# Three plain steps, block sums on the vector engine, and squares summed on the tensor engine in a hybrid decoder layer

## The chip, the cores and the metric

One NeuronCore of a Trainium2 chip runs the kernel in one launch. The metric is the device time of one execution in microseconds. TensorE multiplies, VectorE (DVE) and ScalarE (ACT) work elementwise, GpSimd (POOL) works elementwise too, and SyncE (SP) issues most DMAs. Each engine has its own instruction stream, and the streams meet at semaphores.

## The reference

One layer: a SwiGLU half-step, a mixer, a second SwiGLU half-step and a final RMSNorm, all in float32, for 512 tokens and a model width of 1024.

```python
def rmsnorm(x, w):
    y = x * lax.rsqrt(jnp.mean(x * x, axis=-1, keepdims=True) + EPS)
    return y * w

def swiglu(x, w_gate, w_up, w_down):
    return (jax.nn.silu(x @ w_gate) * (x @ w_up)) @ w_down

x = x + 0.5 * swiglu(rmsnorm(x, ffn1_norm), ...)   # w_gate, w_up: 1024 x 2816
x = x + hybrid_mixer(rmsnorm(x, mix_norm), ...)    # DeltaNet heads and sparse attention heads
x = x + 0.5 * swiglu(rmsnorm(x, ffn2_norm), ...)
y = rmsnorm(x, final_norm)
```

The change touches the start of both feed-forwards and the start of the program. The mixer is only passed through.

## The kernel before

`x` stands transposed in SBUF: 8 tiles k of 128 features by 512 tokens. Every float32 product is made of three passes at full rate: each operand is split into a rounded `hi` and a remainder `lo`, and `three_pass` (lines 572 to 574) adds hi·hi, hi·lo and lo·hi in PSUM. ScalarE makes each `hi` with a copy that rounds, and VectorE each `lo` with a subtraction. For weights these are `act_split_ffn` (L842) and `dve_split_ffn` (L848).

A feed-forward is a fixed list of steps (`ffn_steps`): 22 gate and up steps, each of two output tiles of 128 features, in three parts of 8, 8 and 6, and 4 down steps behind each part. Gate steps have `u` 0, up steps `u` 1. Step s works on half `s % 2` of every ring: the raw weights, `w_hi` and `w_lo`, and four of the eight PSUM banks.

The first `PLAIN` = 2 gate/up steps are **plain**: 2 output tiles by 8 k, 48 products of 128x512. They run on the raw `x` times the norm weights, without the factor 1/rms of each token, which is multiplied into the output later (`dve_plain`, L936). So TensorE can begin before the norm is known. These inputs lie in `act_hi` and `act_lo`, where later the gated result goes.

All other gate/up steps are **block products**: 7 products of half the k by half the tokens in place of 8 (Winograd's form), 84 of 128x256. They need sums of weight blocks, made on GpSimd (`pool_weight_sums`, L862 to L867) and split by ScalarE and VectorE (`act_split_sums` L874, `dve_split_sums` L881), and seven token blocks `hb`: 0, 1, 2 and B12 are quarters of the normed `x` (k low or high, first or second 256 tokens), 3, 4, 5 and 6 sums of them. Each of 0 to 6 is split into `hb_hi` and `hb_lo` of 1024 columns (L667, L671). `hb_hi_home` is the same memory as `hb_hi`, `hb_sum` the same as `hb_lo`, and `w_sum` the same as `w_lo`.

What sets the order at the start of a feed-forward is written out by hand, one list for each engine: `act_ffn_start`, `dve_ffn_start`, `pool_ffn_start`, `pe_ffn_start`. VectorE there makes 16 products of 256 columns for the four quarters (`dve_hr`, L676) and block sum 5 (L716), GpSimd block sums 3, 4 and 6 (L728 to L733) and `hb_lo` 6. VectorE's `hb_lo` 3, 2, 5 and 4 come after the splits of step 2 and the output of step 0. The first block step takes its products in the order 1, 2, 5, 3, 7, 6, 4, which needs the blocks 1, 0, 3, 2, 5, 4, 6. Afterwards `act_ffn`, `dve_ffn` and `pool_ffn` go through the steps, each with the work for the next step's weights ahead of the last step's output.

The norm: ScalarE squares each tile of `x` (L589), GpSimd adds seven of the eight (`pool_sums`, L1017), TensorE sums over the partitions (`pe_norm_sum`, L617), ScalarE takes the root, VectorE the reciprocal, TensorE spreads it over the partitions into bank 7 (`pe_norm_bc`, L630), and ScalarE copies that to `r_sb` (L643). In the first feed-forward, sum and spreading stand behind k = 1 and k = 3 of step 0, in the second behind k = 3 and k = 5.

Before the first product ScalarE and VectorE make, for each k, the square, `act_hi` and `act_lo`; the split of step 0's weights stands ahead of k = 6. ScalarE also issues the DMAs of constants and parameters.

## Time and profile before

| | us |
|---|---|
| median of three timed runs | 1187.64 (1187.3 to 1187.67) |
| the profiled execution's own time | 1181.77 |
| its span | 1180.0 |

| engine | busy us | share |
|---|---|---|
| PE | 1116.3 | 95% |
| PEld | 976.0 | 83% |
| DVE | 783.9 | 66% |
| ACT | 451.1 | 38% |
| POOL | 491.6 | 42% |

The span is the time from the first to the last instruction of the profiled execution. Busy times include no waits. The times of products in the profile overlap, so the distance from the start of one to the start of the next is the better measure of their rate. PEclk is the clock granted to TensorE, as a share of 2.4 GHz.

### The profile page before, as it was taken

What the parts mean: (1) busy time and instruction counts of PE and PEld (TensorE: products, weight loads), DVE (VectorE), ACT (ScalarE), POOL (GpSimd) and SP (SyncE); (2) the same over time, 40 slices, a digit from 0 to 9 for tenths busy, and PEclk for the clock granted to TensorE, in tenths of its full rate; (3) what the DMA queues carried; (4) which work ended last, traced back from release to release, by engine and by line L of the source; (5) the groups of instructions that cost most, each with busy time, mean ns of one, the idle gap of its engine ahead of it and who ended that gap; (6) DMA issues with size and microseconds to landing.
All of it is one profiled execution on the core that took longest, in us unless ns stands there. A gap on an engine that the chain in (4) does not pass through costs nothing.

```text
span 1180.0 us, 20265 instructions
## 1 busy us (share of the span) xinstructions
PE 1116.3 (95%) x8556; PEld 976.0 (83%) x8556; DVE 783.9 (66%) x938; ACT 451.1 (38%) x605; POOL 491.6 (42%) x308
## 2 busy tenths in 40 slices
PE   3889999999999999999999999999599999999996
PEld 2689889988998887877887767887599899989984
DVE  5999458955886566634446387566997379836953
ACT  5444234522434434311124376343543144414431
POOL 3686058704733000313101298423871278306811
PEclk9999999999999999999999899999899999999997
DMA  6223333332332222123111001122133233323221
GB/s 222 67 81 109 106 107 99 103 119 72 108 96 90 95 94 72 38 73 109 37 55 47 8 2 37 37 72 72 65 113 108 75 105 107 119 95 102 74 75 71
DMA packets 33022, 98.45 MB, mean 83 GB/s; under 512 B 3376, under 2 KB 7984, under 8 KB 31280
## 3 DMA queue, kind: packets, MB, share of 16 engines
q1 hardware_dynamic: 31264, 95.95, 24.8%
q10 hardware_dynamic: 1680, 1.39, 0.4%
q8 instruction: 57, 0.93, 0.3%
q14 instruction: 21, 0.17, 0.0%
HBM read 95.24 MB, written 2.10 MB: 82 GB/s over the span
## 4 chain that ended last, share of the span: by engine, by line
PE 85%; DVE 9%; issue 2%; ACT 2%; POOL 1%; DMA 0%; POOLq 0%; DVEq 0%; ACTq 0%
PE bank L572 23%; PE bank L574 23%; PE bank L573 23%; PE bank L1838 3%; DVE hb_lo L671 2%; PE bank L1605 2%; PE bank L1636 2%; PE bank L1621 1%; DVE h_raw L676 1%; PE bank L1896 1%; DVE act_lo L604 1%; DVE w_lo L848 1%; DVE cv L1349 1%; PE bank L617 1%; POOL hb_sum L731 1%
## 5 line engine op out<-in xcount | busy, mean ns | idle before, releaser
L572 PE MATMUL bank<-hb_hi,w_hi 128*128 128x256 f32 x1120 | 316.5, 283 | 22.6 <-DVE hb_lo L671 8.8
L573 PE MATMUL bank<-hb_lo,w_hi 128*128 128x256 f32 x1120 | 315.3, 282 | 0.0
L574 PE MATMUL bank<-hb_hi,w_lo 128*128 128x256 f32 x1120 | 315.3, 282 | 0.0
L572 PEld LDWEIGHTS bank<-hb_hi,w_hi 128*128 128x128 f32 x1120 | 212.3, 190 | 25.8 <-issue 19.9
L573 PEld LDWEIGHTS bank<-hb_lo,w_hi 128*128 128x128 f32 x1120 | 212.4, 190 | 0.2
L574 PEld LDWEIGHTS bank<-hb_hi,w_lo 128*128 128x128 f32 x1120 | 212.5, 190 | 0.0
L572 PE MATMUL bank<-act_hi,w_hi 128*128 128x512 f32 x416 | 166.1, 399 | 20.1 <-DVE w_lo L848 20.1
L842 ACT ACTIVATE w_hi<-raw 128x1536 fp32r<-128x1536 f32 (+1 forms) x68 | 109.8, 1614 | 166.3 <-PE bank L574 162.4
L848 DVE TENSOR_TENSOR w_lo<-raw,w_hi 128x1536 fp32r<-128x1536 f32 (+1 forms) x68 | 163.0, 2397 | 14.2 <-ACT w_hi L842 13.4
L862 POOL TENSOR_TENSOR w_sum<-raw 128x512 f32<-128x512 f32 x40 | 64.4, 1610 | 250.0 <-PE bank L574 250.0
L574 PE MATMUL bank<-act_hi,w_lo 128*128 128x512 f32 x416 | 165.6, 398 | 0.0
L573 PE MATMUL bank<-act_lo,w_hi 128*128 128x512 f32 x416 | 165.6, 398 | 0.0
L881 DVE TENSOR_TENSOR w_lo<-w_sum,w_hi 128x1024 fp32r<-128x1024 f32 x80 | 105.3, 1321 | 30.1 <-POOL w_sum L867 30.1
L874 ACT ACTIVATE w_hi<-w_sum 128x1024 fp32r<-128x1024 f32 x80 | 84.0, 1058 | 85.2 <-POOL w_sum L867 73.7
L572 PEld LDWEIGHTS bank<-act_hi,w_hi 128*128 128x128 f32 x416 | 78.9, 190 | 38.9 <-DVE w_lo L848 20.1
L572 PE MATMUL bank<-h_hi,w_hi 128*128 128x512 f32 x264 | 109.4, 414 | 0.0
L999 DVE SCALAR_TENSOR_TENSOR x<-bank,x 128x512 f32<-128x512 f32 x48 | 30.9, 686 | 111.0 <-PE bank L574 111.0
L574 PE MATMUL bank<-h_hi,w_lo 128*128 128x512 f32 x264 | 104.6, 396 | 0.0
L573 PE MATMUL bank<-h_lo,w_hi 128*128 128x512 f32 x264 | 104.5, 396 | 0.0
L574 PEld LDWEIGHTS bank<-act_hi,w_lo 128*128 128x128 f32 x416 | 78.8, 189 | 19.2
L573 PEld LDWEIGHTS bank<-act_lo,w_hi 128*128 128x128 f32 x416 | 78.9, 190 | 18.7
L865 POOL TENSOR_TENSOR w_sum<-raw 128x512 f32<-128x512 f32 x40 | 94.2, 2354 | 0.0
(282 smaller groups left out, 1767.5 us busy)
## 6 DMA issues: line engine op xcount, KB each, us to landing
raw<-in_gate_up SPq DMA_DIRECT2D x44, 1024.0 KB, 5.3
raw<-in_w_in SPq DMA_DIRECT2D x13, 1024.0 KB, 5.0
raw<-in_down SPq DMA_DIRECT2D x8, 1024.0 KB, 5.2
raw<-in_down SPq DMA_DIRECT2D x16, 512.0 KB, 4.2
raw<-in_down SPq DMA_DIRECT2D x8, 768.0 KB, 4.3
raw<-in_w SPq DMA_DIRECT2D x8, 512.0 KB, 3.9
x<-in_x SPq DMA_DIRECT2D x4, 512.0 KB, 5.9
raw<-in_w_out SPq DMA_DIRECT2D x4, 512.0 KB, 4.9
```

Of the source, the lines that this page charges most:

```text
L572: pe.matmul(out_ap, wh, xh, start=first, stop=False)
L573: pe.matmul(out_ap, wh, xl, start=False, stop=False)
L574: return pe.matmul(out_ap, wl, xh, start=False, stop=last)
L671: eng.tensor_tensor(hb_lo[:, b], HB_RAW[b], hb_hi[:, b].bitcast(F32), ALU.subtract).then_inc(ready, 1)
L842: act.activation(w_hi[:, par, 0:cols], raw[:, par, 0:cols], ACT.Copy).then_inc(hi_ready, 1)
L848: dve.tensor_tensor(w_lo[:, par, 0:cols], raw[:, par, 0:cols], w_hi[:, par, 0:cols].bitcast(F32), ALU.subtract).then_inc(lo_ready, 1)
L862: pool.tensor_tensor(S[0], A[3], A[2], ALU.add).then_inc(s_sum, 1)
L865: pool.tensor_tensor(S[2], A[1], A[3], ALU.subtract).then_inc(s_sum, 1)
L874: act.activation(w_hi[:, par, c], w_sum[:, par, c], ACT.Copy).then_inc(s_hi, 1)
L881: dve.tensor_tensor(w_lo[:, par, c], w_sum[:, par, c], w_hi[:, par, c].bitcast(F32), ALU.subtract).then_inc(s_lo, 1)
L999: dve.scalar_tensor_tensor(x[:, k, :], banks[4 * (st.step % 2) + ab][:, :], 0.5, x[:, k, :], ALU.mult, ALU.add).then_inc(x_added, 1)
L1838: mm = pe.matmul(o[ch, q, :], a, b, start=True, stop=True)
```

## The change

It sets `PLAIN` to 3, so step 2 of each feed-forward is plain too, and the first block step is an up step, number 3, with the banks 4 to 7. The token blocks are written in pairs by 8 products of 512 columns, reading the spread norm from PSUM bank 7, not from `r_sb`. All four block sums and all seven `hb_lo` are VectorE's, and `pool_ffn_start` is gone. The hand-written lists get a new order. ScalarE waits for the end of step 2 before it writes the gated result of steps 0 and 1, since step 2 still reads `act_hi`.

The squares of the first norm are no longer added on GpSimd: TensorE sums each over the partitions, 0 to 5 ahead of the first plain product and 6 and 7 inside step 0. The weights of step 0 are split in two halves (k 0 to 3 and k 4 to 7), behind tile 4. Parameters are issued ahead of the constants, and the rest of the constants goes from ScalarE's DMA queue to SyncE's.

```diff
-PLAIN = 2
+PLAIN = 3
...
-HB_ORDER = (1, 0, 3, 2, 5, 4, 6)
+HB_HI_ORDER = (1, 0, 2, 3, 5, 4, 6)
+HB_LO_ORDER = (1, 3, 2, 0, 5, 4, 6)
...
+            if m == 0:
+                if k >= 2:
+                    act.wait_ge(sq_multiplied, k - 1)
+            elif positive(k + SUMMED0[m] - 1):
...
+        def pe_head_sums(pe, ks):
+            for k in ks:
+                if k == 0:
+                    pe.wait_ge(consts_landed, 16)
+                pe.wait_ge(sq_ready, k + 1)
+                mm = sum_up(pe, sq[:, k % 2, :], k == 0, k == KT - 1)
+                mm.then_inc(ss_ready if k == KT - 1 else sq_multiplied, 1)
...
-        def dve_hr(dve, f, out, k0, tok):
+        def dve_hr(dve, f, out, k0):
             dve.wait_ge(r_ready, 2 * f + 1)
             for k in range(KT // 2):
-                dve.scalar_tensor_tensor(out[:, k, :], x[:, k0 + k, tok], norm_w[:, 2 * f, k0 + k:k0 + k + 1],
-                                         r_sb[:, tok], ALU.mult, ALU.mult).then_inc(h_raw_ready, 1)
+                dve.scalar_tensor_tensor(out[:, :, k, :], x[:, k0 + k, :].rearrange("p (h t) -> p h t", h=2),
+                                         norm_w[:, 2 * f, k0 + k:k0 + k + 1],
+                                         banks[7][:, :].rearrange("p (h t) -> p h t", h=2),
+                                         ALU.mult, ALU.mult).then_inc(h_raw_ready, 1)
 
         def dve_hb(dve, f, b):
-            if b in (2, 3, 4, 5):
-                dve.wait_ge(hb_sum_dve, f + 1)
-                if b > 2:
-                    dve.wait_ge(hb_sum_pool, 3 * f + {3: 1, 5: 2, 4: 3}[b])
-            hb_split(dve, f, b, hb_lo_dve)
+            dve.wait_ge(hb_hi_ready, 7 * f + HB_HI_ORDER.index(b) + 1)
+            if b != 1:
+                dve.wait_ge(hb_sum_dve, 4 * f + {3: 1, 2: 2, 5: 3, 4: 4, 6: 4, 0: 4}[b])
+            dve.tensor_tensor(hb_lo[:, b], HB_RAW[b], hb_hi[:, b].bitcast(F32), ALU.subtract).then_inc(hb_lo_dve, 1)
...
+        def dve_hb_sum(dve, f, b):
+            dve.wait_ge(h_raw_ready, f * KT + (KT // 2 if b == 3 else KT))
+            if b in (4, 6):
+                dve.wait_ge(hb_sum_dve, 4 * f + {4: 2, 6: 3}[b])
+            in0, in1, op = {3: (B12, HB_RAW[1], ALU.subtract), 5: (HB_RAW[2], B12, ALU.subtract),
+                            4: (HB_RAW[1], hb_sum[:, 5], ALU.add), 6: (HB_RAW[0], hb_sum[:, 4], ALU.subtract)}[b]
+            dve.tensor_tensor(hb_sum[:, b], in0, in1, op).then_inc(hb_sum_dve, 1)
...
             act_hb(act, f, 1)
+            act_split_ffn(act, st[2])
             act_hb(act, f, 0)
-            act_split_ffn(act, st[2])
+            act_hb(act, f, 2)
             act_hb(act, f, 3)
-            act_hb(act, f, 2)
-            act_split_sums(act, st[2])
+            act_evac(act, st[0])
             act_hb(act, f, 5)
             act_hb(act, f, 4)
-            act_evac(act, st[0])
+            act_split_ffn(act, st[3])
             act_hb(act, f, 6)
+            act_split_sums(act, st[3])
+            act.wait_ge(step_done, splits(st[2].step) + 1)
+            act_evac(act, st[1])
 
         def dve_ffn_start(dve, f):
 
             st = FFN[f]
-            half = KT // 2
             dve_split_ffn(dve, st[1])
             dve_rstd(dve, 2 * f)
-            dve_hr(dve, f, HB_RAW[1], half, T_LO)
-            dve_hr(dve, f, B12, half, T_HI)
+            dve_hr(dve, f, K_HIGH, KT // 2)
+            dve_hr(dve, f, K_LOW, 0)
             dve_hb(dve, f, 1)
-            dve_hr(dve, f, HB_RAW[0], 0, T_LO)
-            dve_hr(dve, f, HB_RAW[2], 0, T_HI)
+            dve_plain(dve, st[0])
+            dve_split_ffn(dve, st[2])
+            dve_hb_sum(dve, f, 3)
+            dve_hb_sum(dve, f, 5)
+            dve_hb_sum(dve, f, 4)
+            dve_hb_sum(dve, f, 6)
+            dve_hb(dve, f, 3)
+            dve_hb(dve, f, 2)
             dve_hb(dve, f, 0)
-            dve.wait_ge(h_raw_ready, 2 * (f + 1) * KT)
-            dve.tensor_tensor(hb_sum[:, 5], HB_RAW[2], B12, ALU.subtract).then_inc(hb_sum_dve, 1)
-            dve_split_ffn(dve, st[2])
-            dve_plain(dve, st[0])
-            dve_split_sums(dve, st[2], 0)
-            dve_hb(dve, f, 3)
-            dve_split_sums(dve, st[2], 1)
-            for b in (2, 5, 4):
-                dve_hb(dve, f, b)
-
-        def pool_ffn_start(pool, f):
-
-            pool.wait_ge(h_raw_ready, 2 * f * KT + KT)
-            pool.tensor_tensor(hb_sum[:, 3], B12, HB_RAW[1], ALU.subtract).then_inc(hb_sum_pool, 1)
-            pool_weight_sums(pool, FFN[f][2])
-            pool.wait_ge(hb_sum_dve, f + 1)
-            pool.tensor_tensor(hb_sum[:, 4], HB_RAW[1], hb_sum[:, 5], ALU.add).then_inc(hb_sum_pool, 1)
-            pool.wait_ge(hb_sum_pool, 3 * f + 2)
-            pool.tensor_tensor(hb_sum[:, 6], HB_RAW[0], hb_sum[:, 4], ALU.subtract).then_inc(hb_sum_pool, 1)
-            hb_split(pool, f, 6, hb_lo_pool)
+            dve_plain_evac(dve, st[1])
+            dve_split_ffn(dve, st[3])
+            dve_hb(dve, f, 5)
+            dve_split_sums(dve, st[3], 0)
+            dve_gated(dve, st[1])
+            dve_hb(dve, f, 4)
+            dve_hb(dve, f, 6)
+            dve_split_sums(dve, st[3], 1)
+            dve_act_lo(dve, st[1])
 
         def pe_hb_wait(pe, f, b):
-            if b == 6:
-                pe.wait_ge(hb_lo_pool, f + 1)
-            else:
-                pe.wait_ge(hb_lo_dve, 6 * f + HB_ORDER.index(b) + 1)
+            pe.wait_ge(hb_lo_dve, 7 * f + HB_LO_ORDER.index(b) + 1)
...
-            sum_after, bc_after = (1, 3) if f == 0 else (3, 5)
+            bc_after = 3 if f == 0 else 4
+            if f == 0:
+                pe_head_sums(pe, range(HEAD_SUMS + 1))
...
+                if f == 0 and st is FFN[0][0]:
+                    pe.wait_ge(first_lo, 1)
+                else:
+                    pe.wait_ge(lo_ready, splits(st.step) + 1)
+                start = st is FFN[f][0]
+                if st is FFN[f][2]:
+                    pe.wait_ge(post_done, 5 * st.n - 5)
...
+                    if f == 0 and start and t == 1 and k < KT - 1 - HEAD_SUMS:
+                        pe_head_sums(pe, (HEAD_SUMS + 1 + k,))
+                    if f and start and t == 1 and k == 2:
                         pe_norm_sum(pe, m)
-                    if st.u == 0 and t == 1 and k == bc_after:
+                    if start and t == 1 and k == bc_after:
                         pe_norm_bc(pe, m)
...
+        def act_split_first(act):
+            act.wait_ge(raw_landed[0], 16)
+            act.activation(first_half(w_hi, 0), first_half(raw, 0), ACT.Copy).then_inc(first_hi, 1)
+            act.activation(first_half(w_hi, 1), first_half(raw, 1), ACT.Copy).then_inc(hi_ready, 1)
+
+        def dve_split_first(dve):
+            dve.wait_ge(first_hi, 1)
+            dve.tensor_tensor(first_half(w_lo, 0), first_half(raw, 0), first_half(w_hi, 0).bitcast(F32),
+                              ALU.subtract).then_inc(first_lo, 1)
+            dve.wait_ge(hi_ready, 1)
+            dve.tensor_tensor(first_half(w_lo, 1), first_half(raw, 1), first_half(w_hi, 1).bitcast(F32),
+                              ALU.subtract).then_inc(lo_ready, 1)
...
+        def sp_consts(sp):
+            for a, b in KEPT_RUNS[1:]:
+                sp.dma_start(consts[:, KEPT_AT[a][0]:KEPT_AT[b][1]],
+                             dram["consts"][:, CONST_AT[a][0]:CONST_AT[b][1]]).then_inc(rest_landed, 16)
+            for c in range(2):
+                ch = slice(c * CHUNK, (c + 1) * CHUNK)
+                neg, lev = [dram["consts"][ch, CONST_AT[n][0]:CONST_AT[n][1]] for n in COMPACT]
+                sp.dma_start(neg_c[ch], neg[:, ch]).then_inc(compact_landed, 16)
+                sp.dma_start(level_c[ch], lev.rearrange("p (l n) -> p l n", n=P)[:, :, ch])\
+                  .then_inc(compact_landed, 16)
...
+                if f == 0 and i == 8:
+                    sp_consts(sp)
...
         def _(act):
             first = CONST_AT["ones"][1]
+            act.dma_start(params[:, :], dram["params"]).then_inc(params_landed, 16)
             act.dma_start(consts[:, 0:first], dram["consts"][:, 0:first]).then_inc(consts_landed, 16)
-            act.dma_start(params[:, :], dram["params"]).then_inc(params_landed, 16)
             for k in range(KT):
-                if k == KT - 2:
-                    act_split_ffn(act, FFN[0][0])
+                if k == HEAD_SUMS:
+                    act_split_first(act)
                 act_square(act, 0, k)
                 act_hp(act, 0, k)
             act_ffn_start(act, 0)
```

## Rows read from the trace of the kernel before

**Rows 1.** The page, part 4: the chain that ended last, shares of the span by engine.

```profile
PE 85%; DVE 9%; issue 2%; ACT 2%; POOL 1%; DMA 0%; POOLq 0%; DVEq 0%; ACTq 0%
```

**Rows 2.** What TensorE waited for in the whole span: total us, times, longest us.

```profile
PE bank L572 <- DVE w_lo L848: 25.2, 3, 20.1
PE bank L572 <- DVE hb_lo L671: 8.8, 7, 2.8
```

**Rows 3.** Windows: stretch, its us, busy us and instructions by engine, PEclk granted clock, DMA.

```profile
47.20:50.30 3.10, 0.21 (x1) 0.01 (x1) 3.10 (x5) 2.46 (x3) 2.86 (x1) 1.00 0.07 9
50.30:54.60 4.30, 4.28 (x24) 4.17 (x24) 4.30 (x2) 3.28 (x3) 4.20 (x2) 0.65 0.69 237
54.60:69.70 15.10, 8.23 (x61) 7.36 (x60) 15.07 (x10) 4.21 (x6) 12.89 (x6) 0.99 0.29 77
825.50:831.10 5.60, 0.00 (x0) 0.00 (x0) 5.60 (x8) 5.02 (x6) 2.81 (x1) 0.89 0.02 4
831.10:836.30 5.20, 5.12 (x24) 5.15 (x24) 5.20 (x2) 4.13 (x4) 4.25 (x2) 0.50 0.54 199
836.30:851.50 15.20, 8.41 (x62) 7.42 (x61) 15.16 (x9) 4.19 (x6) 13.77 (x7) 0.99 0.00 1
852.00:858.00 6.00, 6.00 (x51) 5.86 (x51) 5.86 (x7) 1.52 (x2) 5.28 (x3) 1.00 0.53 175
```

**Rows 4.** Timeline of VectorE, first feed-forward: start us, us, engine, line, operation, count.

```profile
8.81 7.99 DVE L604 SCALAR_TENSOR_TENSOR act_lo<-x,params,act_hi 128x512 fp32r<-128x512 f32 x5 [0.38 <-ACT act_hi L598]
...
21.33 2.28 DVE L848 TENSOR_TENSOR w_lo<-raw,w_hi 128x2048 fp32r<-128x2048 f32 x1
...
31.21 3.25 DVE L676 SCALAR_TENSOR_TENSOR hb_hi_home<-x,params,r_sb 128x256 f32<-128x256 f32 x8 [3.95 <-ACT r_sb L643]
...
35.52 6.93 DVE L676 SCALAR_TENSOR_TENSOR h_raw<-x,params,r_sb 128x256 f32<-128x256 f32 x4
...
46.15 1.21 DVE L716 TENSOR_TENSOR hb_sum<-hb_sum,hb_hi_home 128x1024 f32<-128x1024 f32 x1
47.28 1.74 DVE L848 TENSOR_TENSOR w_lo<-raw,w_hi 128x1536 fp32r<-128x1536 f32 x1
48.95 1.27 DVE L936 TENSOR_TENSOR c_sb<-bank,r_sb 128x512 f32<-128x512 f32 x2
...
56.72 7.82 DVE L671 TENSOR_TENSOR hb_lo<-hb_sum,hb_hi 128x1024 fp32r<-128x1024 f32 x3
```

**Rows 5.** Timeline of VectorE, second feed-forward.

```profile
812.07 3.26 DVE L676 SCALAR_TENSOR_TENSOR hb_hi_home<-x,params,r_sb 128x256 f32<-128x256 f32 x8 [3.96 <-ACT r_sb L643]
...
848.81 2.85 DVE L848 TENSOR_TENSOR w_lo<-raw,w_hi 128x1536 fp32r<-128x1536 f32 x1
```

**Rows 6.** Timeline of TensorE in step 0 of the first feed-forward.

```profile
20.14 0.80 PE L572 MATMUL bank<-act_hi,w_hi 128*128 128x512 f32 x1 [20.14 <-DVE w_lo L848]
...
24.14 0.46 PE L572 MATMUL bank<-act_hi,w_hi 128*128 128x512 f32 x1
...
24.90 0.94 PE L617 MATMUL bank<-consts,sq_sum 128*128 128x1 f32 x8
...
26.60 0.48 PE L572 MATMUL bank<-act_hi,w_hi 128*128 128x512 f32 x1
...
28.78 0.40 PE L572 MATMUL bank<-act_hi,w_hi 128*128 128x512 f32 x1
29.02 0.39 PE L573 MATMUL bank<-act_lo,w_hi 128*128 128x512 f32 x1
```

**Rows 7.** Timeline of ScalarE before the first product; ACTq is its DMA issue.

```profile
0.75 0.40 ACTq L2228 DMA_DIRECT2D consts<-in_consts  x1
...
6.92 0.72 ACT L598 ACTIVATE act_hi<-x,params 128x512 fp32r<-128x512 f32 x1 [1.38 <-DMA params<-in_params]
...
8.07 0.71 ACT L598 ACTIVATE act_hi<-x,params 128x512 fp32r<-128x512 f32 x1
...
14.15 1.90 ACT L842 ACTIVATE w_hi<-raw 128x2048 fp32r<-128x2048 f32 x1
```

**Rows 8.** DMA issues from 0 to 0.9 and 2.6 to 2.9 us: KB, us to landing.

```profile
consts<-in_consts ACTq DMA_DIRECT2D x1, 65.0 KB, 4.3
...
raw<-in_gate_up SPq DMA_DIRECT2D x1, 1024.0 KB, 9.8
```

**Rows 9.** The page, part 5: an operation of VectorE with one PSUM operand.

```profile
L999 DVE SCALAR_TENSOR_TENSOR x<-bank,x 128x512 f32<-128x512 f32 x48 | 30.9, 686 | 111.0 <-PE bank L574 111.0
```

More of the change, by code:

```diff
@@ L574, in three_pass @@
             return pe.matmul(out_ap, wl, xh, start=False, stop=last)
-        SUMMED0 = [m * (KT - 1) for m in range(4)]
+        SUMMED0 = [0] + [m * (KT - 1) for m in range(3)]
+        HEAD_SUMS = 5
         def x_there(m, k):
@@ L793, in gate_up @@
                 def gate_up(i):
-                    if part == 0 and isinstance(i, int) and i == 0:
-                        return
                     for st in ups[:2]:
-                        first = part == 0 and st.u == 0 and isinstance(i, int) and i == PLAIN // 2
+                        first = part == 0 and isinstance(i, int) and 2 * i + st.u == PLAIN
+                        if part == 0 and isinstance(i, int) and 2 * i + st.u < PLAIN:
+                            continue
                         pe.wait_ge(lo_ready, i * 2 + (splits(st.step) + 1))
@@ L1005, in pool_ffn @@
         def pool_ffn(pool, f):
-            pool_ffn_start(pool, f)
-            for st in FFN[f][PLAIN + 1:]:
+            for st in FFN[f][PLAIN:]:
                 if summed(st):
```

87 lines of the change are left out of this document (36 added, 51 removed).

## The prediction

> **What bounds the kernel now.** The chain of waits by engine comes first: TensorE 85%, VectorE 9% [rows 1]. TensorE is the bound, and the chain leaves it where it idles. TensorE's waits say where: 25.2 us for the split weights `w_lo`, 20.1 of them before its first product, and 8.8 us for `hb_lo` [rows 2]. The windows say when [rows 3]. Two stretches are badly filled: 47.2 to 69.7 us, at the start of the first feed-forward, and 825.5 to 851.5 us, at the start of the second. In each one block-product step is done. Such a step has 84 products; 51 started in 6.00 us, 0.118 us each, 9.9 us in all. So of 22.5 us in the first stretch 12.6 are lost, and of 26.3 us (825.3 to 851.6) in the second 16.4. With the late start that is nearly all of TensorE's waiting for VectorE. In both stretches VectorE is busy throughout. The clock adds: after 5.6 us without a product the granted clock was 0.50, which is the 1.2 GHz level, and 24 products took 5.2 us (0.217 each, 2.3 us lost); after 3.1 us idle it was 0.65 on average [rows 3].
>
> **How VectorE's time is made up.** VectorE runs at two prices. With GpSimd idle an operation with both tensors in SBUF takes 1.13 us for 1024 columns (from the start at 46.15 to the next at 47.28) and 1.67 us for 1536. With GpSimd busy, three of 1024 took 7.82 us, 2.6 each; four of 256 columns took 6.93 us, where eight had taken 3.25; the split of 1536 took 2.85 instead of 1.74 [rows 4, 5]. So one GpSimd operation costs VectorE between 1.11 (2.85 - 1.74) and 1.47 us (2.6 - 1.13). I take 1.11, as its row has the 512-column weight sums on GpSimd that will be left. A read from PSUM is not lengthened: two of 512 took 1.27 us amid busy GpSimd [rows 4].
> The Trainium skill, page "SBUF — State Buffer", section "Who interferes with whom", gives the rule: an operation of VectorE with two SBUF inputs and one of GpSimd that reads SBUF shut each other out for a whole instruction, and one with at most one SBUF input is left alone. The trace agrees (2.6 against 1.13 us, and 1.27 us for the two from PSUM). It speaks against this change at one place, since the sums of the first two block steps stay on GpSimd and meet the longest VectorE queue.
>
> **Start of the first feed-forward.** Now the first product starts at 20.14 us [rows 6]. ScalarE's products with the norm weights begin at 6.92, when the parameters landed [rows 7]; VectorE needs 7.99 us for five `act_lo`, with GpSimd adding squares beside it [rows 4]. After: the parameters are issued first. What is first now, at 0.75, took 4.3 us to land, so they land between 5.0 and 6.9 us [rows 7, 8]; I take 6.4. Five rounds of square and product at 1.13 us (6.92 to 8.07 between products [rows 7]) end at about 11.5. The raw weights land at 12.5 (issued at 2.66, 9.8 us [rows 8]), and bound the split: ScalarE does halves of 1024 columns in 0.95 us (half of 1.90 [rows 7]), at 13.5 and 14.4, and VectorE its first half by 14.8. But TensorE must first sum the squares 0 to 5, and square 5 is issued behind both halves: ready at 15.0. Its sum is half of the sixteen records that took 1.70 us (24.90 to 26.60), 0.85 us at the clock of that stretch, twice this at 1.2 GHz [rows 6]. Start 15.9 to 16.7, I take 16.2. Gain 3.9 us. The first nine products now take 4.0 us (20.14 to 24.14), 0.44 each against 0.235 later (28.78 to 29.02), so 1.9 us are lost [rows 6]. Whether sums with one column raise the clock beforehand no row shows: bounds 0 and 1.9 us more gain. I take 0, since waits lie between the sums.
> The sums for squares and the broadcast inside step 0 cost what they did (1.7 and 0.85 us). Step 0 then ends at 16.2 + 11.3 + 1.9 + 2.5 = 31.9 and step 1 at 43.2, against 47.2.
>
> **First feed-forward, steps 2 to 4.** A plain step has 48 products of 0.235 us: 11.3 us, 1.4 more than a block step. In it TensorE waits for nothing, as its weights are split at about 36.4. VectorE's queue: the broadcast norm is in PSUM after k=3 of step 0, 25.9, copied at 26.5 (now 31.2 [rows 4]). Eight products of 512 columns with one PSUM operand cost 0.65 each by the row of 686 ns [rows 9], less the overlap: 5.2 us, against 16 of 256 in now 12.8 us. They end at 31.7; `hb_lo` 1 at 32.9, step 0's output (two from PSUM, 1.2) at 34.1, the weights of step 2 (2.28 [rows 4]) at 36.3, four block sums (4 x 1.14) at 40.9, `hb_lo` 3 and 2 at 43.2. Here GpSimd starts on the sums of step 3, as its buffer is free at the end of step 1. From there: `hb_lo` 0, output of step 1, weights of step 3, `hb_lo` 5, weight-sum split 0, gate product, `hb_lo` 4 and 6, weight-sum split 1: nine entries, 10.8 us of their own (1.13 + 1.25 + 1.67 + 6 x 1.13), and four waits for the sums of step 3 up to 52, then two for those of step 4 (6 x 1.11 = 6.7 us, of which some 0.9 fall beside the PSUM reads). Last split at 59.8. TensorE: step 2 to 54.4, products 1, 2, 5 of step 3 to 58.6, product 3 waits for this split 1.2 us, step 3 ends at 65.4. Its weights for step 4 are then split (65.0). Now step 4 starts at 69.7 + 9.9 = 79.6. Gain 14.2 us, the 3.9 included.
>
> **Second feed-forward.** Norm sum and broadcast come after k=2 and k=4 instead of 3 and 5: one k is 6 products, 1.4 us, so VectorE begins at 810.7, not 812.1 [rows 5]. Step 0 ends as now at 814.0 and step 1 at 825.3, for TensorE comes here without a pause. The same queue: eight products to 815.9, `hb_lo` 1 817.0, output 0 818.3, weights of step 2 820.5, four sums 825.1. It is here 2.2 us further behind step 1's end than in the first feed-forward, so all three `hb_lo` meet GpSimd. The nine entries and `hb_lo` 3 and 2 are 10.8 + 2.3 = 13.1 us, with seven waits of 1.11 20.9: last split at 846.0. TensorE has finished step 2 at 836.6 and products 1, 2, 5 at 840.8: it stalls 5.2 us. That is as long as the 5.6 us after which the clock fell, so 2.3 us more [rows 3]. Its last four products take 5.6, and step 3 ends at 853.9, where now step 4 starts at 851.6 + 9.9 = 861.5: gain 7.6 us.
> **Later steps.** VectorE's work between two weight splits stays what it is (about 9 of 9.9 us), and weights of step 4 are ready before TensorE wants them; I add 0, with 2 us as the other end. The 1.1 MB of constants go from ScalarE's queue to SyncE's, ahead of the raw weights of step 8. SyncE waits there for most of a step, so seven issues of 0.5 us are hidden, the transfer too; without that cover some 3 us. ScalarE loses those issues, worth nothing while it is idle.
>
> **Sum.** 14.2 + 7.6 = 21.8 us from the profiled execution's 1181.77, which gives 1160.0. The median shown is 1187.64, 5.9 above it, and I take the same difference: 1165.9 us.
>
> **Rivals.**
> A. *The second stall is missing*: if GpSimd's sums cost VectorE nothing, seven waits (7.8 us) go, TensorE has no stall and no slow clock in the second feed-forward (5.2 + 2.3 more) and 1.2 less in the first, and with a warm start 1.9: gain 30.5 to 32.4, about 1156 us. Against it: the 2.6 us of [rows 4]. Half of it, if GpSimd's operations come mainly beside PSUM reads: 1161.
> B. *The queue on VectorE gets longer*: at 1.47 us a wait, 13 waits cost 4.7 us more, and steps 4 and 5 start late by 1 us each time: gain 15.1, 1172.5. For it: VectorE has no idle time before either.
> C. *The start is not earlier* because sums at 1.2 GHz hold ScalarE's two square buffers: six at 1.7 us from 6.5 end at 16.7, worth 0.5; with parameters or `ones` landing late, up to 2: 1168.
> D. *Slower*: the sums moved to VectorE become the bound. It takes over three block sums, one `hb_lo` and 512 more weight columns, 5.1 us for each feed-forward. If what slows VectorE in the rows is not GpSimd but its own SBUF traffic, eight products at 1.73 instead of 0.65 and six operations at 2.25 instead of 1.13 add 15.3 us to each queue: 30.6 - 21.8 = 8.8 slower, 1196.4. It decides from about 10.8 us of added queue. Against it: the same operation at 1.13 us with GpSimd idle.
> E. *The change does not do what it says*: in the second feed-forward the squares still go through GpSimd, so there it only moves the norm; that is counted.
>
> **Numbers.** Forecast 0.52, A or its half 0.20, B 0.18, C 0.05, D 0.03, nothing much 0.02. The range 1157.5 to 1174.5 takes in A's nearer part and B. The forecast's own is 1162 to 1170. What a measurement of this kernel can tell from no change is about 0.2%, 2.4 us: faster 0.94, same 0.03, slower 0.03.
>
> **What would show it.** First product near 16.2 us; no idle time of TensorE in step 2 of either feed-forward; VectorE's eight norm products in 5.2 us, block sums at 1.14 each; a wait for `w_lo` from `w_sum` (about 5 us) in the second feed-forward's first block step and about 1 in the first's, with a clock near 0.5 behind the long one. I am wrong if the first product comes after 18 us, if TensorE waits for `hb_lo` there, or if a wait of over 2 us appears in steps 4 to 7.

## The result and the profile after

The changed kernel takes 1173.1 us (median of four, 1170.7 to 1177.3), the kernel before 1187.5 in the same series: ratio 0.989, 95% interval 0.9866 to 0.9913. (Ratios and intervals here are estimated over all executions, so they differ a little from the quotient of the medians.) A second series gave 1173.7 against 1190.1, ratio 0.9875 (0.9846 to 0.9903). It is faster, by 14.4 us where 21.8 were forecast. That is inside the stated range, but 7.2 us above the point and outside the 1162 to 1170 us that the forecast's own terms gave; it is the number of rival B, 1172.5.

The profiled execution took 1177.34 us, the slowest of its series. Its chain of waits by engine, to be read beside [rows 1]:

```profile
PE 89%; DVE 5%; issue 2%; ACT 2%; POOL 1%; DMA 0%; POOLq 0%; DVEq 0%; ACTq 0%
```

What TensorE waited for in the whole span, as total, number of times and longest, beside [rows 2]. The line numbers are the changed kernel's: L917 is the split of weight sums, L621 the sums of squares.

```profile
PE bank L574 <- DVE w_lo L917: 8.4, 2, 5.3
PE bank L621 <- ACT sq L595: 8.0, 2, 7.6
```

VectorE's share of the chain fell from 9 to 5%. All waits for `hb_lo` are gone, and so is the wait of 20.1 us for the first weights. In its place stands one of 7.6 us ahead of the first sum of squares. In the two feed-forwards there are two waits for the second weight-sum split, 3.1 and 5.3 us, one in each.

**The head.** TensorE's timeline ahead of and in step 0 of the first feed-forward, beside [rows 6]; the columns are start and length in us:

```profile
7.57 8.70 PE L621 MATMUL bank<-consts,sq 128*128 128x1 f32 x40 [7.57 <-ACT sq L595]
16.66 1.87 PE L621 MATMUL bank<-consts,sq 128*128 128x1 f32 x8 [0.39 <-ACT sq L595]
18.39 0.77 PE L574 MATMUL bank<-act_hi,w_hi 128*128 128x512 f32 x1
...
30.48 0.58 PE L576 MATMUL bank<-act_hi,w_lo 128*128 128x512 f32 x1
30.90 0.40 PE L574 MATMUL bank<-act_hi,w_hi 128*128 128x512 f32 x1
31.13 0.39 PE L575 MATMUL bank<-act_lo,w_hi 128*128 128x512 f32 x1
```

Forty records of one-column sums took 8.70 us, 1.74 us for each tile of `x`, and so did the sum of square 5. The first product came at 18.39, not 16.2. The products of step 0 stood 0.43 us apart up to 30.48, and 0.23 from 30.90 on: 12 us at 1.2 GHz, where the kernel before had 4. The constants, with the column of ones, were issued second, and landed 6.4 us after their issue at 1.17, which is 7.57, the very start of the first sum, beside [rows 8]. So the sum waited for them, and not for the square that the row names, which ScalarE had made by 6.43.

```profile
params<-in_params ACTq DMA_DIRECT2D x1, 172.5 KB, 5.2
consts<-in_consts ACTq DMA_DIRECT2D x1, 65.0 KB, 6.4
```

**VectorE in both feed-forwards**, beside [rows 4, 5]; its timeline, the last two lines from the second one:

```profile
33.32 2.72 DVE L681 SCALAR_TENSOR_TENSOR hb_hi_home<-x,params,bank 128x512 f32<-128x512 f32 x4 [5.75 <-ACT r_sb L655]
35.95 2.72 DVE L681 SCALAR_TENSOR_TENSOR hb_sum<-x,params,bank 128x512 f32<-128x512 f32 x4
...
59.00 1.23 DVE L917 TENSOR_TENSOR w_lo<-w_sum,w_hi 128x1024 fp32r<-128x1024 f32 x1 [1.26 <-POOL w_sum L903]
...
61.28 4.56 DVE L690 TENSOR_TENSOR hb_lo<-hb_sum,hb_hi 128x1024 fp32r<-128x1024 f32 x2
65.77 2.28 DVE L917 TENSOR_TENSOR w_lo<-w_sum,w_hi 128x1024 fp32r<-128x1024 f32 x1
...
842.20 4.52 DVE L690 TENSOR_TENSOR hb_lo<-hb_sum,hb_hi 128x1024 fp32r<-128x1024 f32 x2
846.64 2.28 DVE L917 TENSOR_TENSOR w_lo<-w_sum,w_hi 128x1024 fp32r<-128x1024 f32 x1
```

Eight norm products take 5.3 us (33.32 to 38.59, 5.2 forecast). `hb_lo` 4 and 6 take 2.28 us each, not 1.13, since GpSimd is at its sums, and the last split another 2.28. In the first feed-forward VectorE even stands idle for 1.26 us ahead of 59.00, for the last of GpSimd's four sums.

TensorE behind the stall of the second feed-forward:

```profile
848.98 0.58 PE L574 MATMUL bank<-hb_hi,w_hi 128*128 128x256 f32 x1 [5.28 <-DVE w_lo L917]
849.35 0.42 PE L575 MATMUL bank<-hb_lo,w_hi 128*128 128x256 f32 x1
```

and windows of the first plain products, of step 2 and of the products behind that stall, with the same columns as [rows 3]:

```profile
18.30:30.20 11.90, 11.90 (x38) 10.06 (x38) 3.97 (x4) 4.64 (x6) 0.00 (x0) 1.00 0.58 178
49.60:60.80 11.20, 11.20 (x50) 9.04 (x49) 9.94 (x8) 4.58 (x5) 9.15 (x4) 1.00 0.08 12
848.90:853.40 4.50, 4.42 (x20) 4.43 (x21) 4.37 (x6) 1.89 (x3) 0.00 (x0) 0.50 0.01 2
```

Step 2 (49.6 to 60.8) has TensorE busy throughout. Behind the stall 20 products take 4.5 us at a clock of 0.50. In the head the same column prints 1.00 although the products stand 0.43 us apart: there the distances must be read, not PEclk.

### The profile page after: what moved, and what is told of

The parts are those of the page before. It is cut to its first block, busy times and chain, and to the rows that moved or that the text cites. A ratio compares the mean times of both kernels' runs of the same rounds, so it can differ in the third digit from the quotient of the medians.

```text
span 1175.5 us, 20165 instructions
## 1 busy us (share of the span) xinstructions
PE 1137.8 (97%) x8532; PEld 993.8 (85%) x8532; DVE 761.5 (65%) x921; ACT 447.8 (38%) x600; POOL 442.6 (38%) x284
## 4 chain that ended last, share of the span: by engine, by line
PE 89%; DVE 5%; issue 2%; ACT 2%; POOL 1%; DMA 0%; POOLq 0%; DVEq 0%; ACTq 0%
PE bank L574 24%; PE bank L575 23%; PE bank L576 23%; PE bank L1890 3%; PE bank L1657 2%; PE bank L1688 2%; PE bank L621 1%; PE bank L1673 1%; DVE hb_lo L690 1%; PE bank L1948 1%; PE bank L1937 1%; PE bank L1944 1%; PE bank L1942 1%; PE bank L1496 1%; PE bank L1316 0%
## 5 line engine op out<-in xcount | busy, mean ns | idle before, releaser
L574 PE MATMUL bank<-hb_hi,w_hi 128*128 128x256 f32 x1064 | 299.8, 282 | 8.4 <-DVE w_lo L917 8.4
L575 PE MATMUL bank<-hb_lo,w_hi 128*128 128x256 f32 x1064 | 299.6, 282 | 0.0
L576 PE MATMUL bank<-hb_hi,w_lo 128*128 128x256 f32 x1064 | 299.6, 282 | 0.0
L574 PEld LDWEIGHTS bank<-hb_hi,w_hi 128*128 128x128 f32 x1064 | 202.0, 190 | 9.1 <-DVE w_lo L917 8.8
L575 PEld LDWEIGHTS bank<-hb_lo,w_hi 128*128 128x128 f32 x1064 | 201.9, 190 | 0.3
L576 PEld LDWEIGHTS bank<-hb_hi,w_lo 128*128 128x128 f32 x1064 | 202.0, 190 | 0.0
L898 POOL TENSOR_TENSOR w_sum<-raw 128x512 f32<-128x512 f32 x38 | 59.0, 1553 | 332.8 <-PE bank L576 332.8
L574 PE MATMUL bank<-act_hi,w_hi 128*128 128x512 f32 x448 | 179.9, 402 | 0.0
L575 PE MATMUL bank<-act_lo,w_hi 128*128 128x512 f32 x448 | 179.2, 400 | 0.0
L576 PE MATMUL bank<-act_hi,w_lo 128*128 128x512 f32 x448 | 179.2, 400 | 0.0
L868 DVE TENSOR_TENSOR w_lo<-raw,w_hi 128x1536 fp32r<-128x1536 f32 (+1 forms) x67 | 159.1, 2374 | 15.2 <-ACT w_hi L862 14.4
L917 DVE TENSOR_TENSOR w_lo<-w_sum,w_hi 128x1024 fp32r<-128x1024 f32 x76 | 101.2, 1336 | 31.0 <-POOL w_sum L903 30.9
L910 ACT ACTIVATE w_hi<-w_sum 128x1024 fp32r<-128x1024 f32 x76 | 80.2, 1058 | 95.6 <-POOL w_sum L903 81.7
L1039 DVE SCALAR_TENSOR_TENSOR x<-bank,x 128x512 f32<-128x512 f32 x48 | 30.9, 686 | 111.0 <-PE bank L576 111.0
L901 POOL TENSOR_TENSOR w_sum<-raw 128x512 f32<-128x512 f32 x38 | 91.8, 2415 | 0.0
```

Source lines behind the costliest of these rows:

```text
L574: pe.matmul(out_ap, wh, xh, start=first, stop=False)
L575: pe.matmul(out_ap, wh, xl, start=False, stop=False)
L576: return pe.matmul(out_ap, wl, xh, start=False, stop=last)
L868: dve.tensor_tensor(w_lo[:, par, 0:cols], raw[:, par, 0:cols], w_hi[:, par, 0:cols].bitcast(F32), ALU.subtract).then_inc(lo_ready, 1)
L898: pool.tensor_tensor(S[0], A[3], A[2], ALU.add).then_inc(s_sum, 1)
L901: pool.tensor_tensor(S[2], A[1], A[3], ALU.subtract).then_inc(s_sum, 1)
```

## Where the time went: three stretches in several profiles

One event each marks the end of step 3 of the first feed-forward (ScalarE's split of step 5's weights, which can't begin before it), the beginning of the second (its split of the weights of step 1), and the end of step 4 of the second (its split for step 6). ScalarE's timeline has them; in the third profile of the kernel before the first two are:

```profile
81.18 1.49 ACT L842 ACTIVATE w_hi<-raw 128x1536 fp32r<-128x1536 f32 x1
...
811.67 1.90 ACT L842 ACTIVATE w_hi<-raw 128x2048 fp32r<-128x2048 f32 x1
```

| profile | execution, us | to the end of step 3 | from there to the second feed-forward | from there to the end of its step 4 |
|---|---|---|---|---|
| before, first | 1181.8 | 80.2 | 723.1 | 68.7 |
| before, second | 1184.3 | 80.0 | 726.8 | 68.7 |
| before, third | 1193.3 | 81.2 | 730.5 | 71.5 |
| changed, first | 1177.3 | 75.6 | 730.5 | 60.9 |
| changed, second | 1170.4 | 70.3 | 730.0 | 60.7 |

The last column fell by 7.8 and 8.0 us from its value in the first two profiles of before (7.6 forecast). The first fell by 4.6 or 9.9 us, where 14.2 were forecast. In the last row ScalarE was late: TensorE began step 4 at 69.27 us there, against 79.95 in the first profile of before, so the gain was 10.7 us; elsewhere in the table the first mark lies 0.3 to 0.4 us behind TensorE. The middle column, in which neither kernel differs but for the DMA queue of the constants, goes from 723 to 730 us in the kernel before alone. A kernel that differs from the changed one in one operand (experiment 9) has 724.1 us there, so the change does not fix that stretch at 730 either. The first profile of before, on which the prediction stood, was the fastest of the three, so the two first profiles' difference (4.4 us) says little. The two gains add up to 12.4 us in the one profile and 18.7 in the other, around the 14.4 of the medians.

## The experiments

All but the kernels before are edits of the changed kernel. The time is a median over the executions of its series, with their least and greatest, and the ratio is to the kernel before in the same series; where only one execution was made, it says so.

**1. The changed kernel again.** No edit.

> The changed kernel once more, for a second profile beside the first. In the first profile the mixer, between about 344 and 677 us, took 6.6 us longer than in the kernel before, though nothing in it was changed. Theory (the difference is the clock's, which falls at other moments from execution to execution): this profile shows another length of that stretch, by some us, while the first feed-forward's start is the same within 2 us. Rival (the change reaches into the mixer, by the constants that SyncE now loads or by its phase): the stretch is again 6 to 7 us longer. Time: 1173 us, 1170 to 1177.

1173.7 us (1170.4 to 1176.7), ratio 0.9875 (0.9846 to 0.9903). TensorE's head in this profile:

```profile
20.96 1.02 PE L621 MATMUL bank<-consts,sq 128*128 128x1 f32 x8
21.84 0.48 PE L574 MATMUL bank<-act_hi,w_hi 128*128 128x512 f32 x1
22.16 0.40 PE L575 MATMUL bank<-act_lo,w_hi 128*128 128x512 f32 x1
```

The clock rose between 20.96 and 21.84 us here, at 30.9 in the first profile, with the same instructions ahead of it. Block step 3 began at 56.0 us instead of 60.6: 4.6 us. Then there is a second difference, behind the same stall of 3.1 us. Windows of 4.5 us from TensorE's next product on, in the first profile and in this one:

```profile
68.10:72.60 4.50, 4.50 (x25) 4.50 (x26) 4.37 (x4) 0.88 (x1) 1.08 (x1) 0.62 0.00 0
```

```profile
63.50:68.00 4.50, 4.47 (x38) 4.47 (x39) 4.37 (x4) 0.84 (x1) 1.12 (x1) 1.00 0.00 0
```

The clock fell behind the stall in the first profile and stayed here, which is 1.5 us more. So TensorE began step 4 at 75.4 us there and at 69.3 here; "the same within 2 us" was wrong. The later profiles show which case is the rule. Of the seven with this head and no added products ahead of the first plain one (the changed kernel twice, experiments 5 to 9), two have the rise at 21 us and five at 30 to 31. The four with the head of before (experiment 3 among them) have it at 24 to 26. The middle stretch was again 6.9 us over the first profile of before, so the rival had to be taken seriously, and the kernel before was profiled twice more.

**2. The kernel before, second and third profile.** No edit.

> The kernel before once more, for a second profile. Its first profile came from an execution of 1181.8 us, while its median is 1187 to 1190; it has no fall of the clock near 580 and 640 us, and five profiles of changed kernels have both. Theory (those falls come and go with the execution, whatever the kernel): this profile, if its time is near the median, shows a granted clock below 1 near 580 and 640 us and a stretch from the last weights of the first feed-forward to the second feed-forward that is 5 to 8 us longer than in the first profile. Rival (the change brings the falls): the stretch is the same as in the first profile within 1 us, and an execution near the median is longer elsewhere.

> The kernel before, a third profile. The second one, 1184.3 us, was longer than the first only in the mixer (3.2 us by 604 us, with a fall of the clock near 590 that the first lacks), and equal to it within 0.5 us in both feed-forwards. Theory: both feed-forwards are again the same within 1 us, and an execution near the median of 1188 us has its difference of 4 to 8 us in the mixer. Rival: the feed-forwards of before differ as well, and then a comparison of single profiles of them says little.

1184.3 and 1193.3 us. The second has 3.7 us more in the mixer, not the 5 to 8 expected, and a fall of the clock near 594 us but none near 640: neither the theory nor its rival as written. It has nothing more elsewhere; the third, unchanged code, has the whole 7.4 us, and 2.8 more in the second feed-forward. So the longer mixer comes and goes without the change. The third profile also refutes "both feed-forwards are the same within 1 us".

**3. The old head.**

```diff
-        SUMMED0 = [0] + [m * (KT - 1) for m in range(3)]
+        SUMMED0 = [m * (KT - 1) for m in range(4)]
...
-            if f == 0:
-                pe_head_sums(pe, range(HEAD_SUMS + 1))
...
-                    if f and start and t == 1 and k == 2:
+                    if start and t == 1 and k == (2 if f else 1):
...
+            pool_sums(pool, 0)
...
-                if k == HEAD_SUMS:
-                    act_split_first(act)
+                if k == KT - 2:
+                    act_split_ffn(act, FFN[0][0])
...
```

> The changed kernel with the head of the program as before: squares added on GpSimd, norm sum behind k=1 of step 0, weights of step 0 split in one piece ahead of tile 6, constants issued ahead of parameters. Theory (one-column sums ran at 1.7 us a tile because TensorE was at 1.2 GHz, and they kept it there until 30.5 us): the first product comes at 20.1 us instead of 18.4, but the clock rises 4 us later, step 1 ends at 47.2 instead of 49.7, and the kernel is 2 to 3 us faster than the changed one, 1170.5. Rival (the late landing of the constants, 7.6 us, is what cost the head its gain, and the clock plays no part): 1.7 us slower than the changed one, 1175.

1170.8 us (1170.0 to 1173.2), ratio 0.985 (0.9824 to 0.9877), 2.9 us under the changed kernel of the same series (1173.7). The first product comes at 20.24, 2 us later, and TensorE begins step 4 at 73.5, 1.9 us before the first profile of the changed kernel and 4.2 behind its second. The time varies over 3.2 us, the changed kernel's over 6.4. The clock rose at 25 us, behind 4.8 us of slow TensorE. The intervals of the two ratios overlap, so that the old head is faster by 2.9 us is not shown; what the series speaks against is the rival, by which it is slower. By the profiles, what the new head wins at the first product it pays at the clock in five of seven executions, and not in the other two.

**4. Dense products ahead of the sums.**

```diff
+        def pe_warm(pe, n):
+            src = z[:, 0, :].bitcast(BF16)
+            for _ in range(n):
+                pe.matmul(banks[7][:, :], src[:, 0:P], src[:, P:P + SEQ], start=True, stop=True)
+
         def pe_head_sums(pe, ks):
             for k in ks:
+                if k == 0:
+                    pe.wait_ge(warm_set, 1)
+                    pe_warm(pe, 20)
...
                 mm.then_inc(ss_ready if k == KT - 1 else sq_multiplied, 1)
+                if k == 4:
+                    pe_warm(pe, 8)
```

> The changed kernel with 20 dense products on a cleared tile ahead of the first sum of squares and 8 behind the fifth; their result is not used. Theory (clock): the sums take 0.85 us a tile, the first product comes at about 16 us and runs at 0.235 us from the start; step 1 ends near 41.5 us instead of 49.7, of which the VectorE queue behind it gives back a part: 5 to 8 us faster than the changed kernel, 1166.5. Rival (constants and raw weights bound the head): the first product stays at 18.4 us and only its 4.3 us of slow products go: 3 to 4 us, 1169. Second rival (a fall of the clock in the head does not depend on what TensorE does there): no change, 1173.

1170.3 us (1164.4 to 1175.4), ratio 0.9833 (0.9798 to 0.9869): 3.4 us under the changed kernel by the medians, with intervals that overlap, and not the 7 expected. TensorE's timeline, and windows of it from 8 us on:

```profile
1.35 6.16 PE L629 MATMUL bank<-z 128*128 128x512 bf16 x20 [1.35 <-POOL z L2280]
7.51 5.97 PE L622 MATMUL bank<-consts,sq 128*128 128x1 f32 x40
13.71 3.19 PE L629 MATMUL bank<-z 128*128 128x512 bf16 x7 [0.24 <-issue]
16.70 1.71 PE L622 MATMUL bank<-consts,sq 128*128 128x1 f32 x8
18.27 0.77 PE L575 MATMUL bank<-act_hi,w_hi 128*128 128x512 f32 x1
```

```profile
8.00:10.00 2.00, 2.00 (x19) 2.00 (x19) 0.81 (x2) 1.43 (x4) 0.00 (x0) 1.00 1.05 389
10.00:12.00 2.00, 1.84 (x14) 1.67 (x14) 1.44 (x2) 2.00 (x4) 0.00 (x0) 0.90 0.99 334
12.00:14.00 2.00, 1.76 (x8) 1.59 (x10) 0.94 (x2) 1.44 (x3) 0.00 (x0) 0.50 0.90 369
```

The dense products did what they should: the five sums behind them take 5.97 us, 1.2 each, ScalarE's pace. But in the midst of the sums the clock fell, 0.90 and then 0.50, though TensorE was busy for 1.84 of 2.00 us. The 8 dense products then ran at half speed and delayed the sixth sum to 16.70, though ScalarE had its square at 15.24, and the first product came at 18.27 all the same. So in this execution one-column sums did not keep the clock up, as the theory has it, and in none of the other profiles had some 10 us of them raised it by the first product. The second rival, a fall that has nothing to do with what TensorE does, is made unlikely by experiment 10 and not excluded. That 28 dense products would repair the head was wrong.

**5. Dense products in the stalls.**

```diff
+                if first and p == 3:
+                    for _ in range(10 if st.f == 0 else 36):
+                        pe.matmul(banks[3][:, 0:TOK], w_hi[:, par, 0:P], hb_hi[:, 1, 0, :], start=True, stop=True)
                 if p in S_PART:
```

> The changed kernel with dense products into an unused bank ahead of the wait for the second weight-sum split: 10 in the first feed-forward (1.2 us of the 3.1 us stall), 36 in the second (4.3 of 5.3 us). Their result is not used. Theory (a stall of that length makes the clock fall, and that costs 1.6 and 2.3 us): the stall in the second feed-forward shrinks to about 1 us, the products behind it run at 0.118 us instead of 0.213, and 2 us are gained in the second, 0 to 1.6 in the first: 1170.5. Rival (the slow products behind the stall come from something else, such as VectorE's writes): same time as the changed kernel, 1173.

1171.3 us (1160.9 to 1173.3), ratio 0.9828 (0.9791 to 0.9866), 2.4 us less than the changed kernel by the medians, which is not clear of the noise; the profile has to decide. TensorE's first two products behind the wait of the second feed-forward, and its wait there:

```profile
846.30 0.39 PE L574 MATMUL bank<-hb_hi,w_hi 128*128 128x256 f32 x1 [1.09 <-DVE w_lo L920]
846.52 0.28 PE L575 MATMUL bank<-hb_lo,w_hi 128*128 128x256 f32 x1
```

```profile
PE bank L574 <- DVE w_lo L920: 1.1, 1, 1.1
```

The wait is 1.1 us, the clock stays, and the last column of the table becomes 59.0, 1.9 us less. In the first feed-forward 10 products filled 1.2 of 3.1 us, and nothing was gained: the clock fell there all the same. The slow products of the second feed-forward belong to the idle time, as forecast: the clock falls behind the stall of 5.3 us in every profile that has it (both of the changed kernel, experiments 3, 4 and 9), and in none of those where it is filled or gone (here, 7 and 10). Behind the 3.1 us of the first it fell in four of five. The time is TensorE's alone; VectorE's queue is as long as it was.

**6. The second split first.**

```diff
             dve_split_sums(dve, st[3], 0)
+            dve_split_sums(dve, st[3], 1)
-            dve_gated(dve, st[1])
             dve_hb(dve, f, 4)
             dve_hb(dve, f, 6)
-            dve_split_sums(dve, st[3], 1)
+            dve_gated(dve, st[1])
             dve_act_lo(dve, st[1])
```

> The changed kernel with VectorE's second weight-sum split of step 3 directly behind the first, ahead of hb_lo 4 and 6 and the gate product. Theory (VectorE's whole queue from the norm to the weights of step 4 is the bound, not the one entry that TensorE waits for): the wait in step 3 goes in both feed-forwards, but the weights of step 4 are split no earlier than before (73.3 and 853.1 us), TensorE waits 5 to 6 us for them, and the clock falls behind that wait: 1 to 3 us faster than the changed kernel, 1171.5. Rival (only the order of the entries is wrong): both stalls (8.4 us) and their slow products (3.9 us) go: 1162.

1174.5 us (1167.3 to 1177.4), ratio 0.9885 (0.9849 to 0.9922): no gain, where 1171.5 was expected. TensorE's only wait at the start of the second feed-forward:

```profile
PE bank L574 <- DVE w_lo L868: 6.6, 1, 6.6
```

L868 is the split of step 4's weights. The wait for the sums is gone, and one of 6.6 us for the next step's weights has taken its place; in the first feed-forward it is 3.2 us, where 3.1 went. The entry that TensorE waited for was not the bound; VectorE's queue as a whole is.

**7. GpSimd's next sums later.**

```diff
             for st in FFN[f][PLAIN:]:
+                if st is FFN[f][PLAIN + 1]:
+                    pool.wait_ge(s_lo, 2 * FFN[f][PLAIN].s + 2)
```

> The changed kernel, but GpSimd begins the weight sums of step 4 only when VectorE has split all sums of step 3. Theory (each GpSimd operation costs VectorE 1.1 us in that queue): hb_lo 4 and 6 and the second split take 1.13 us each instead of 2.25, the stall falls from 5.3 to about 1 us in the second feed-forward and from 3.1 to 0 in the first, the clock stays up behind both, and step 4 starts some 6.8 and 4.5 us earlier; 11 us faster than the changed kernel, 1162. Rival (what is not paid now is paid in step 4, whose sums come later and meet VectorE then): the stalls go, but TensorE waits for sums inside step 4: 2 to 4 us faster, 1170.

1166.8 us (1163.2 to 1170.0), ratio 0.983 (0.9797 to 0.9863): 6 to 7 us under the changed kernel's two medians, where 11 were expected. VectorE in the second feed-forward, and TensorE's waits there:

```profile
835.31 2.35 DVE L690 TENSOR_TENSOR hb_lo<-hb_sum,hb_hi 128x1024 fp32r<-128x1024 f32 x2
837.58 1.22 DVE L917 TENSOR_TENSOR w_lo<-w_sum,w_hi 128x1024 fp32r<-128x1024 f32 x1
...
841.27 2.81 DVE L868 TENSOR_TENSOR w_lo<-raw,w_hi 128x1536 fp32r<-128x1536 f32 x1
...
846.58 2.23 DVE L917 TENSOR_TENSOR w_lo<-w_sum,w_hi 128x1024 fp32r<-128x1024 f32 x1 [1.84 <-POOL w_sum L903]
```

```profile
PE bank L574 <- DVE w_lo L868: 1.4, 1, 1.4
PE bank L574 <- DVE w_lo L917: 1.0, 1, 1.0
```

`hb_lo` 4 and 6 now take 1.13 us each and the split 1.14, with nothing changed on VectorE. That is the price of GpSimd's operations shown by itself: 1.14 us for each entry (2.28 - 1.14). The Trainium skill has the rule for it in "SBUF — State Buffer", section "Who interferes with whom": an operation of VectorE with two SBUF inputs contends with one of GpSimd that reads SBUF. The trace agrees (2.28 against 1.14 us). The rival has its part: the weights of step 4 take 2.81 us, VectorE idles 1.84 us for the late sums, and TensorE waits 1.4 and 1.0 us. The last column of the table is 56.2, 4.6 us less. In the first feed-forward TensorE begins step 5 at 77.6 us, against 79.1 in the second profile of the changed kernel, which has the same head: 1.5 us. Together that is 6.1, near the 6 to 7 measured; TensorE begins step 4 3.1 us earlier and loses half of it there again.

**8. Two block sums on GpSimd again.**

```diff
-            dve_hb_sum(dve, f, 4)
-            dve_hb_sum(dve, f, 6)
...
+            pool.tensor_tensor(hb_sum[:, 4], HB_RAW[1], hb_sum[:, 5], ALU.add).then_inc(hb_sum_pool, 1)
+            pool.wait_ge(hb_sum_pool, 2 * f + 1)
+            pool.tensor_tensor(hb_sum[:, 6], HB_RAW[0], hb_sum[:, 4], ALU.subtract).then_inc(hb_sum_pool, 1)
```

> The changed kernel with block sums 4 and 6 on GpSimd again; all else, the third plain step too, is kept. Theory (a sum that goes to GpSimd saves VectorE 1.13 us but shuts it out for the 2 to 2.5 us that GpSimd needs for 1024 columns): hb_lo 3, 2 and 0 take 2.2 to 3.3 us each, the last weight-sum split comes 2 to 4 us later in each feed-forward, and the kernel is 4 to 7 us slower than the changed one, 1179. Rival (a second engine helps, since VectorE is the bound): 2 x 2.3 us faster, 1168.5.

1178.0 us (1174.0 to 1183.7), ratio 0.9925 (0.9897 to 0.9952), 4.3 to 4.9 us slower than the changed kernel's two medians. VectorE, then GpSimd, in the second feed-forward:

```profile
828.48 4.57 DVE L694 TENSOR_TENSOR hb_lo<-hb_sum,hb_hi 128x1024 fp32r<-128x1024 f32 x2
835.46 2.21 DVE L694 TENSOR_TENSOR hb_lo<-hb_sum,hb_hi 128x1024 fp32r<-128x1024 f32 x1 [2.40 <-POOL hb_sum L1050]
```

```profile
828.63 3.34 POOL L1048 TENSOR_TENSOR hb_sum<-hb_hi_home,hb_sum 128x1024 f32<-128x1024 f32 x1 [19.93 <-DVE hb_sum L700]
832.05 3.27 POOL L1050 TENSOR_TENSOR hb_sum<-hb_sum 128x1024 f32<-128x1024 f32 x1
```

Two sums take GpSimd 6.6 us, 3.3 each, and not 2 to 2.5; VectorE spends 2.28 us on each `hb_lo` beside them and idles 2.40 more for the last. The stall becomes 6.1 us in both feed-forwards, and TensorE begins step 4 2.9 and 2.8 us later than in the first profile of the changed kernel. So the move of these two sums to VectorE is worth some 5 us of the change. What the move of the third sum and of `hb_lo` 6 is worth was not measured.

**9. The norm from SBUF.**

```diff
-                                         banks[7][:, :].rearrange("p (h t) -> p h t", h=2),
+                                         r_sb.rearrange("p (h t) -> p h t", h=2),
```

> The changed kernel with the eight norm products of each feed-forward reading the copy of the spread norm in SBUF and not the PSUM bank. Theory (an operand's place matters only while GpSimd works, and it is idle there): eight products in 5.1 to 5.8 us instead of 5.4, the rest of the timeline as in the changed kernel within 0.6 us. Rival (reading PSUM is what makes them fast): 1.1 us or more each, 4 us later in both feed-forwards.

One execution, 1170.8 us. The first four of the eight products:

```profile
33.24 2.74 DVE L681 SCALAR_TENSOR_TENSOR hb_hi_home<-x,params,r_sb 128x512 f32<-128x512 f32 x4 [5.83 <-ACT r_sb L655]
```

2.74 us against 2.72, and TensorE begins step 4 at 75.3 us against 75.4. With GpSimd idle the place of the operand does not matter here. The gain of this part comes from eight instructions in place of sixteen and from GpSimd's silence, not from PSUM. How much each of the two gives no run separates; in [rows 4] four products of 256 columns take 6.93 us beside GpSimd where eight take 3.25 without it.

**10. The better version.** The edits of experiments 3 and 7 together, and 14 dense products between the fourth `act_lo` and the first product:

```diff
+                pe.wait_ge(warm_set, 1)
+                pe.wait_ge(h_ready, 4)
+                src = z[:, 0, :].bitcast(BF16)
+                for _ in range(14):
+                    pe.matmul(banks[7][:, :], src[:, 0:P], src[:, P:P + SEQ], start=True, stop=True)
```

> Old head (squares on GpSimd, one split), late sums of step 4 as in pool_late, and 14 dense products on a cleared tile between the fourth act_lo and the first product, whose result is not used. Theory (one-column sums count as idleness for the clock, dense products as work): the first product stays at 20.2 us and runs at 0.235 us at once, 1.9 us less than the old head alone, so that this is 11 + 3 + 2 us faster than the changed kernel: 1157.5. Rival (the clock in the head does not follow what TensorE did just before): no gain over the sum of the other two, 1160; and where the clock is late, up to 1.5 us lost at the first product.

1164.1 us (1160.6 to 1168.5), ratio 0.9811 (0.9778 to 0.9843). TensorE:

```profile
13.48 4.91 PE L779 MATMUL bank<-z 128*128 128x512 bf16 x14 [13.48 <-DVE act_lo L608]
20.02 0.50 PE L575 MATMUL bank<-act_hi,w_hi 128*128 128x512 f32 x1 [1.64 <-DVE w_lo L866]
20.36 0.40 PE L576 MATMUL bank<-act_lo,w_hi 128*128 128x512 f32 x1
20.60 0.40 PE L577 MATMUL bank<-act_hi,w_lo 128*128 128x512 f32 x1
```

The first product comes at 20.02 and the products stand 0.23 us apart from the second on. By the medians it beats both kernels, by 24 us the one before and by about 9 the changed one, though by less than forecast, mainly since experiment 7 gave 6 to 7 us and not 11. The intervals of experiments 7 and 10 overlap, so what the dense products and the old head add to the late sums is seen in the profile only: step 1 of the first feed-forward ends at 45.3 us, against 49.4 and 44.8 in the two of the changed kernel.

## Why the prediction came out as it did

The time was inside the stated range, but partly by luck: the range was made wide for rivals A and B, and the 7.2 us that are missing come from other terms than B's. By the profiles they lie in the first feed-forward, which gained 4.6 us in one and 10.7 in the other, for 14.2. One of the prediction's three signs of being wrong came true as well: the first product came after 18 us.

- **Second feed-forward: right, and for its reasons.** Forecast 7.6 us, measured 7.8. The last split waited as forecast behind GpSimd's operations; stall 5.2 forecast, 5.3 measured; slow products behind it 2.3 forecast, and 20 at 0.22 us in place of 0.118 make 2.1. Experiments 5, 7 and 8 show the clock, the price of one GpSimd operation and what it does to VectorE's queue.
- **"I take 16.2" for the first product: mis-sized.** The step priced only the last of six sums, and let ScalarE's rounds run at 1.13 us. The sums ran at 1.74 us a tile at 1.2 GHz and held ScalarE through its two buffers of squares. They also began at 7.57, since the constants landed 0.7 us behind the latest time considered. It came at 18.4. Rival C described the sums, at 0.5 us, and the late `ones`, at up to 2; it was 2.2.
- **"1.9 us are lost", the slow first products: the largest miss, and not a fixed one.** The first profile has 12 us of slow TensorE in step 0, the second 3; the kernel before has 4. Of the 6.2 us that step 0 ended late in the first profile (38.1 against 31.9), 2.2 are the start and 4.0 this; in the second it ended at 33.6, only 1.7 late, though the first product came 2.1 late. The bounds were 0 and 1.9 us of *gain*, and left a loss out, although sums inside step 0 were part of the change. That these sums are what delays the rise fits the profiles (21 or 30 to 31 us with them, 24 to 26 with the old head), but no run took them alone out of step 0, so it is argued and not shown.
- **"Product 3 waits 1.2 us": mis-sized.** 3.1 us. From the first norm product to the last split VectorE took 34.7 us and not 33.3; the 1.26 us in which it waited for GpSimd's last sum stood in no term. Behind so long a wait the clock fell in four of five profiles, which cost 1.5 us more in the first one and stood in no term either.
- **Later steps and constants: right.** TensorE has no wait in steps 4 to 7 and none for the constants.
- **The same difference to the median: sound, as it turned out.** The profile of before lay 5.7 us under its median, and had the shortest mixer of the three profiles. The gain was carried over to the median, as it should be; it was the gain that was too large. The changed kernel's first profile lay 4.2 us above its own median, so the difference of the two profiles would have misled by 10.
- Rival A (no second stall) and D (VectorE as a new bound, slower) did not come about. B gave nearly the measured number, but its mechanism, 1.47 us for each wait, did not: an entry beside GpSimd costs 1.14 more.

What stays open: why the clock rises at 21 us in one execution and at 30 to 31 in another. Its moment was not steered by an experiment, only prepared ahead of the first product in the last one. Nor was the third plain step tried by itself, as the lists of all engines hang on it; that TensorE stands busy through it, and VectorE's queue runs beside, is seen in the profile alone.

## What to carry to other kernels

When work is moved to TensorE to relieve another engine, price it at both of its clocks and ask whether it keeps the clock up: the sums with one column did not here (1.00 at 8 us, 0.50 from 12 us on in experiment 4), and they ran at half speed, 1.74 us a tile, just where they were needed. Where one engine's queue is late, moving the awaited entry forward only moves the wait; shorten the queue, or move what slows it, as GpSimd's sums here. And take two or three profiles of a kernel before a difference of a few microseconds is read from one.
